# Branch a's prompt halves and three modulation tiles placed anew among four attention pairs of a decoder layer

## The chip, the cores and the metric

The kernel runs on one core of one Trainium2 chip. The metric is the device time of one execution in microseconds; the median of three runs stands for the kernel.

## The reference

One layer of a decoder, for a prompt of 256 tokens and for 8 samples of 8 new tokens that have 1024 cached tokens each. In short:

```python
mod = silu(c) @ w_ada + b_ada                       # sh1, sc1, gt1, sh2, sc2, gt2: 6 x 1024 columns
h = rmsnorm(x, g_mix) * (1 + sc1) + sh1
z = h @ w_in                                        # q, k, v, index q/k/w, retention q/k/v/gate, ga, gb
a_out = attend(...)                                 # top-k sparse attention; sample: past cache + new keys
r_out, r_state = retain(...)                        # retention, its new state is an output
merged = sigmoid(ga) * (a_out @ w_pa) + sigmoid(gb) * (r_out @ w_pb)
x = x + gt1 * (merged @ w_o)
x = x + gt2 * moe(rmsnorm(x, g_ffn) * (1 + sc2) + sh2)   # 32 experts, top 4, 12 MB of weights each
y = rmsnorm(x, g_final)
```

Branch a is `a_out @ w_pa`, branch b is `r_out @ w_pb`. All data are float32; the masks of the sample's attention are bfloat16.

## The kernel before

The program is written by hand for each engine: every engine has its own list of instructions in a fixed order, and semaphores tie the lists together. Nothing is reordered by a scheduler; the order of the code is the order of each engine and of each DMA queue. Nearly all loads are issued by SyncE, so a wait in SyncE's list holds up every load behind it.

Weights outside the experts come in tiles of 2 MB (128 partitions by 4096 words), numbered n in the order of their use: 0 to 3 modulation, 4 to 16 the input projection, 17 and 19 to 25 modulation, 18 branch a's weights (`wa`), 26 and 27 the output projection. The tiles share two buffers, `wt[0]` and `wt[1]`, in turn (`slot(n)`); `wa` lies in `wt[0]`, tiles 17, 19, 20 and 22 lie in `wt[1]`. The semaphore `tile_done` counts the matmul groups that have used a tile, in TensorE's order; `load_tile(n)` (L381 to L384) waits for this count before it overwrites a buffer. `w_here[0]` and `w_here[1]` tell TensorE that a tile has landed.

Names that the steps touch:

- `modulation_tile(n, b)` (matmuls at L1236): 16 matmuls of 512 columns (8 steps of k in 4 groups of rows that end in 32 rows each), into PSUM bank b. VectorE copies the bank into `partB[...]` (L1969 for tiles 17 and 19, L2011, `modulation_out`, for the others) and counts `partb_done`.
- `branch_a_prompt(i)` (L1248, L1249): half i (512 of 1024 columns) of branch a for the 256 prompt tokens, into banks 6 and 7. VectorE multiplies the result by the gate (L1974) and counts `ya_done`.
- `branch_a_sample()` (L1258): branch a for the 64 sample tokens, into banks 0 and 1. VectorE multiplies by the gate in four products (L2017), which also count `ya_done`.
- The sample's attention runs in four pairs i of samples. Each pair has, on TensorE, `sample_scores(i)` (L1281, and L1290 for the masks) into banks 0 to 2; `sample_prob_transposes(i)` (L1299, L1300) into banks 3, 4 and 2; `sample_values(i)` (L1313) into bank 5; and `sample_rows(i)` (L1265), a transpose of the pair's output. VectorE takes the maximum (L1961), ScalarE the exponential (L770, it counts `sexp_done`), VectorE copies the transposed probabilities (L1979, L1980, `spt_done`) and divides the output (L1987, `so_done`), ScalarE copies the output rows (L761, L762, `sa_done`).
- The scores of pair i + 1 are issued between the transposes and the values of pair i. At the head of each pair stands a piece of other work: before the change tile 17 for pair 0, branch a's half 0 for pair 1, half 1 for pair 2, tile 19 for pair 3. Tiles 17 and 19 use bank 3, so the pair's transposes wait for VectorE's copy of it.
- After the last pair follow branch a's sample half, tile 20, and then branch b (`project`, L933 to L938), whose first matmuls wait for VectorE's products on banks 0 and 1 (`ya_done` 3).

SyncE's list around this place: the load of tile 17; eight stores of the new retention state (`ret_sample`, L446), each two waiting for a count of `ns_done`; the load of tile 18, `wa`; after the first scores (`ssc2_done` 1) eight loads of 64 KB, the keys of batch row 6 (L356); tile 19; branch b's weights in two parts of 2 MB (L456), each after a pair's scores and values; tile 20; further loads that wait for the last pair. GpSimd gathers the values of the eight batch rows by indirect DMA (L582); rows 4 to 7 land where the stored state lies, so they wait for the stores (`st_out`). ScalarE issues the keys of batch row 7 in two halves, after the exponentials of pairs 0 and 1.

The expert stage streams the weights of 32 experts, six pieces of 2 MB each, through six buffers. A piece of the next expert is issued (L479, L482) when TensorE has used up the buffer (`chunk_used`).

Of the kernel before, what the change touches and what calls it, by code (L numbers as in the profile page):

```python
# [29 lines left out]
PAIRS = DB // 2  # L30
# [4 lines left out]
BANK = 512  # L35
# [111 lines left out]
def kern(nc, a):  # L147
    with ExitStack() as ctx:
# [24 lines left out]
        def bank(b, n=1):  # L173
            return ps[:, b * BANK:(b + n) * BANK]

        z3 = z[:, :].rearrange("p (t n) -> p t n", t=3)
# [185 lines left out]
        def _(sp):  # L362
# [17 lines left out]

            def load_tile(n, src, dst=None):  # L381

                sp.wait_ge(tile_done, n - 1 if n < 26 else n - 2)
                sp.dma_start(wt[slot(n)] if dst is None else dst, src).then_inc(w_here[slot(n)], 16)  # L384

            def load_modulation(n, i):
                load_tile(n, in_tile("w_ada", i))
# [52 lines left out]
            load_keys(sp, 4)  # L440
            load_keys(sp, 5)
            load_modulation(17, 4)

            for b in range(DB):
                sp.wait_ge(ns_done, b // 2 + 1)
                sp.dma_start(a["ret_sample"][b].rearrange("h d v -> d h v"),  # L446
                             state[64 * (b % 2):64 * (b % 2) + 64, b // 2, :, :]).then_inc(st_out[b // 4], 16)
            load_tile(18, a["w_branch_a"].rearrange("p (c n) -> p c n", c=4), wa)
            sp.wait_ge(ssc2_done, 1)
            load_keys(sp, 6)  # L450
            load_modulation(19, 5)
# [445 lines left out]
        def _(pe):  # L897
# [18 lines left out]
            for i in range(4):  # L916
                pe.wait_ge(w_here[i] if i < 2 else side_here[i - 2], 16)
                for k in range(KT):
                    g = k % 4
# [310 lines left out]
            def modulation_tile(n, b):  # L1230

                w = wt[slot(n)] if n < 25 else w_last
                pe.wait_ge(*tile_here(n))
                for k in range(KT):
                    g = k % 4
                    last = nc.tensor.matmul(bank(b)[32 * g:32 * g + 32, :], cT3[:, k, :], w[:, k, :],  # L1236
                                            start=k < 4, stop=k >= 4)
                last.then_inc(tile_done, 1)

            def branch_a_prompt(i):  # L1240

                if i:
                    pe.wait_ge(ya_done, 1)
                else:
                    pe.wait_ge(*tile_here(18))
                for k in range(4):
                    w = wa[:, k, i * BANK:(i + 1) * BANK]
                    nc.tensor.matmul(bank(6), aT3[:, k, 0:P], w, start=k == 0, stop=k == 3)  # L1248
                    last = nc.tensor.matmul(bank(7), aT3[:, k, P:SEQ], w, start=k == 0, stop=k == 3)  # L1249
                last.then_inc(ya_mm, 1)  # L1250
# [16 lines left out]
            def sample_scores(i):  # L1267

                pe.wait_ge(keys_here[i], 64 * NPAGES)
                if i:  # L1270
                    pe.wait_ge(sexp_done, i)
                else:
                    pe.wait_ge(z_done, NZT)
                blocks = ((0, BANK), (1, BANK), (2, DS))
                for k, w in blocks:
                    if i and k == 2:
                        pe.wait_ge(spt_done, i)
                    for h in range(2):
                        b = 2 * i + h
                        keys = kT[b][:, k * BANK:k * BANK + w] if k < 2 else kTn[:, SEQ + b * DS:SEQ + (b + 1) * DS]  # L1280
                        nc.tensor.matmul(bank(k)[NS * h:NS * h + NS, 0:w], z3[:, 2, CQ + b * NS:CQ + (b + 1) * NS],  # L1281
                                         keys, start=True, stop=False)
                if i == 0:
                    pe.wait_ge(masks_done, 1)
                    pe.wait_ge(rep_done, DB)
                    pe.wait_ge(vnew_here, 16 * DB)
                for k, w in blocks:
                    for h in range(2):
                        b = 2 * i + h
                        last = nc.tensor.matmul(bank(k)[NS * h:NS * h + NS, 0:w], rep_b[0:NS, b * NS:(b + 1) * NS],  # L1290
                                                mask_s[0:NS, k * BANK:k * BANK + w], start=False, stop=True)
                last.then_inc(ssc2_done, 1)

            def sample_prob_transposes(i):
                pe.wait_ge(sexp_done, i + 1)
                if i in (0, PAIRS - 1):
                    pe.wait_ge(partb_done, 1 + i // 3)
                for n in range(8):
                    nc.tensor.transpose(bank(3 + n // 4)[:, (n % 4) * P:(n % 4 + 1) * P], p_s[:, n:PAST:8], ident)  # L1299
                nc.tensor.transpose(bank(2)[0:DS, P:2 * P], p_s[:, PAST:KEYS], ident).then_inc(spt_tr, 1)  # L1300
# [17 lines left out]
            for i in range(PAIRS):  # L1318
                if i:
                    pe.wait_ge(spt_done, i)  # L1320
                else:
                    pe.wait_ge(rows_done, 6)
                if i in (0, PAIRS - 1):
                    modulation_tile(17 + 2 * (i // 3), 3)
                else:
                    branch_a_prompt(i - 1)
                if i:
                    sample_rows(i - 1)
                sample_prob_transposes(i)
                if i + 1 < PAIRS:  # L1330
                    sample_scores(i + 1)
                sample_values(i)
            sample_rows(PAIRS - 1)

            pe.wait_ge(sa_done, PAIRS)
            branch_a_sample()
            modulation_tile(20, 6)
            def merged_transposes(half):
                for t in range(3):
                    n = TOK[t]  # L1340
# [299 lines left out]
        def _(dve):  # L1640
# [323 lines left out]
            sample_max(0)  # L1964
            for i in range(PAIRS):

                if i in (0, PAIRS - 1):
                    dve.wait_ge(tile_done, 18 + i // 3)
                    nc.vector.tensor_copy(partB[i // 3], bank(3)).then_inc(partb_done, 1)  # L1969
                else:  # L1970
                    dve.wait_ge(ya_mm, i)
                    for t in range(2):
                        g = z3[:, t, CGA + (i - 1) * BANK:CGA + i * BANK]
                        last = nc.vector.tensor_tensor(g, bank(6 + t), g, ALU.mult)  # L1974
                    last.then_inc(ya_done, 1)
                dve.wait_ge(spt_tr, i + 1)
                if i:
                    dve.wait_ge(spv_done, i)
                nc.vector.tensor_copy(pT_s[:, 0:8, :], bank(3, 2).rearrange("p (n q) -> p n q", q=P))  # L1979
                nc.vector.tensor_copy(pT_s[0:DS, 8, :], bank(2)[0:DS, P:2 * P]).then_inc(spt_done, 1)  # L1980
                step(nc.vector.reciprocal(rs[:, i % 2:i % 2 + 1], rs[:, i % 2:i % 2 + 1]))
                if i + 1 < PAIRS:
                    sample_max(i + 1)
                dve.wait_ge(spv_done, i + 1)
                if i:
                    dve.wait_ge(sa_tr, i)
                nc.vector.tensor_scalar(o_s, bank(5)[:, 0:P], rs[:, i % 2:i % 2 + 1], None, ALU.mult).then_inc(so_done, 1)  # L1987
# [22 lines left out]
                dve.wait_ge(tile_done, 19 + i)  # L2010
                nc.vector.tensor_copy(partB[i], bank(6 + i % 2)).then_inc(partb_done, 1)  # L2011

            dve.wait_ge(tile_done, 20)
            for i in range(2):
                for h in range(2):
                    g = z3[0:NS, 2, CGA + i * BANK + h * 256:CGA + i * BANK + (h + 1) * 256]
# [310 lines left out]
```

## Time and profile before

| | us |
|---|---|
| median of 3 runs | 1473.34 |
| lowest and highest run | 1467.64, 1477.7 |
| the profiled execution's own time | 1471.61 |
| its span, first to last instruction | 1469.8 |
| TensorE busy | 1403.6 (95%) |
| VectorE busy | 512.4 (35%) |
| ScalarE busy | 218.9 (15%) |
| GpSimd busy | 69.8 (5%) |

The span is what the trace covers; the profiled execution's own time is a little longer. Busy times are sums of instructions, so an engine with a small share can still be the one that is waited for at some place. TensorE's granted clock over the span was 0.987 of its full speed. Times in the views are counted from the start of the span. In the views PE is TensorE, DVE is VectorE, ACT is ScalarE, POOL is GpSimd; SPq is SyncE's queue of DMA issues.

### The profile page before, as it was taken

Reading aid. Unit: us, or ns where it says so; the run is one execution under the profiler, and the core shown is the slowest. Engines: PE = TensorE matmul, PEld = TensorE weight load, DVE = VectorE, ACT = ScalarE, POOL = GpSimd, SP = SyncE. Lnnn points to the kernel's source line nnn. Section 1 sums busy time; section 2 is a strip of 40 time slices with the busy share of each in tenths; the row PEclk is TensorE's granted clock in tenths of the full one; section 3 lists DMA queues with packets and bytes.
Section 4 is the critical chain, followed back from the end, with each engine's and each line's share of the span. In section 5 each row is a group of like instructions: output and inputs, shape, how many; then the busy total and the mean of one; then the engine's idle time right before and its main releaser. Section 6 shows DMA issues by size and latency. Waiting matters only on the chain.

```text
span 1469.8 us, 17354 instructions
## 1 busy us (share of the span) xinstructions
PE 1403.6 (95%) x6581; PEld 584.9 (40%) x6581; DVE 512.4 (35%) x1090; ACT 218.9 (15%) x403; POOL 69.8 (5%) x67
## 2 busy tenths in 40 slices
PE   6999999998999899999999999999999999999995
PEld 3544556554445633333333333333333333333331
DVE  5133895762221522332232233213312332233125
ACT  2111222112002120111111111101111111011112
POOL 1002501141000100000000000000000000000000
PEclk9999999999999999999999999999999999999998
DMA  9424254249647369999999999999999999999992
GB/s 393 137 80 145 89 150 143 94 144 363 271 158 311 136 273 429 428 427 428 429 429 428 429 429 429 429 428 428 429 429 428 429 429 428 429 429 429 428 428 104
DMA packets 61578, 487.70 MB, mean 332 GB/s; under 512 B 8246, under 2 KB 30070, under 8 KB 32730
## 3 DMA queue, kind: packets, MB, share of 16 engines
q1 hardware_dynamic: 59226, 482.35, 79.7%
q0 software_dynamic: 1152, 4.19, 0.8%
q8 instruction: 29, 0.48, 0.1%
q10 hardware_dynamic: 1152, 0.52, 0.1%
q14 instruction: 19, 0.16, 0.0%
HBM read 482.93 MB, written 4.08 MB: 331 GB/s over the span
## 4 chain that ended last, share of the span: by engine, by line
DMA 36%; PE 34%; DVE 2%; issue 1%; ACT 0%; SPq 0%; DVEq 0%
DMA ring<-in_w_gate_up 36%; PE ps L1564 16%; PE ps L1605 5%; PE ps L1393 2%; PE ps L1511 2%; PE ps L1542 1%; PE ps L933 1%; PE ps L934 1%; PE ps L1557 1%; PE ps L1236 0%; PE ps L1348 0%; PE ps L937 0%; PE ps L1499 0%; PE ps L1587 0%; PE ps L1519 0%
## 5 line engine op out<-in xcount | busy, mean ns | idle before, releaser
L1564 PE MATMUL ps<-ring,z 128*64 128x512 f32 x2048 | 451.3, 595 | 21.1 <-DMA ring<-in_w_gate_up 21.1
L1564 PEld LDWEIGHTS ps<-ring,z 128*64 128x64 f32 x2048 | 142.2, 137 | 328.0 <-issue 278.0
L2174 DVE TENSOR_SCALAR actT<-ps 128x512 f32<-128x512 f32 x32 | 22.1, 691 | 612.6 <-PE ps L1564 612.6
L1605 PE MATMUL ps<-ring,z 128*64 128x512 f32 x1024 | 226.0, 594 | 0.0
L1605 PEld LDWEIGHTS ps<-ring,z 128*64 128x64 f32 x1024 | 72.0, 137 | 149.7 <-issue 145.5
L954 PE MATMUL ps<-ring,actT 128*128 128x512 f32 (+1 forms) x208 | 105.2, 587 | 0.0
L955 PE MATMUL ps<-ring,actT 128*128 128x512 f32 (+1 forms) x208 | 103.8, 580 | 0.0
L1511 PE MATMUL ps<-z,actT 128*64 128x512 f32 x384 | 90.6, 607 | 0.0
L1542 PE MATMUL ps<-z,aT 128*128 128x512 f32 x128 | 67.8, 631 | 2.8 <-ACT z L862 1.2
L2144 DVE TENSOR_TENSOR xr<-xr,z 128x512 f32<-128x512 f32 (+1 forms) x80 | 63.8, 797 | 2.7
L2136 DVE TENSOR_TENSOR z<-ps,z 128x512 f32<-128x512 f32 x64 | 44.1, 689 | 47.6 <-PE ps L1542 47.6
L849 ACT ACTIVATE actT<-actT 128x512 f32<-128x512 f32 x32 | 20.0, 626 | 258.9 <-DVE actT L2174 258.9
L955 PEld LDWEIGHTS ps<-ring,actT 128*128 128x128 f32 x208 | 39.5, 190 | 47.3 <-issue 45.9
L861 ACT ACTIVATE z<-ps 64x512 f32<-64x512 f32 x32 | 18.9, 589 | 248.5 <-PE ps L1605 248.5
L954 PEld LDWEIGHTS ps<-ring,actT 128*128 128x128 f32 x208 | 38.0, 190 | 41.5 <-issue 39.8
L968 PE MATMUL ps<-ring,actT 128*64 128x256 f32 (+1 forms) x208 | 46.4, 376 | 0.0
L967 PE MATMUL ps<-ring,actT 128*64 128x256 f32 (+1 forms) x208 | 46.4, 376 | 0.0
L1511 PEld LDWEIGHTS ps<-z,actT 128*64 128x64 f32 x384 | 26.6, 139 | 48.3 <-issue 47.3
L1788 DVE MAX8 st<-ring 64x8 f32<-64x1032 f32 (+2 forms) x48 | 45.0, 937 | 1.4
L1789 DVE MATCH_REPLACE8 ring<-st,ring 64x1032 f32<-64x1032 f32 (+2 forms) x48 | 44.1, 920 | 0.0
L842 ACT ACTIVATE aT<-ps 128x320 f32<-128x320 f32 x16 | 7.0, 437 | 225.5 <-PE ps L1527 225.5
L1393 PE MATMUL ps<-actT,ring 128*128 128x320 f32 x128 | 36.6, 439 | 0.0
(345 smaller groups left out, 1232.8 us busy)
## 6 DMA issues: line engine op xcount, KB each, us to landing
ring<-in_w_gate_up SPq DMA_DIRECT2D x128, 2048.0 KB, 22.9
ring<-in_w_down SPq DMA_DIRECT2D x64, 2048.0 KB, 20.6
ring<-in_w_in SPq DMA_DIRECT2D x12, 2048.0 KB, 7.8
ring<-in_w_ada SPq DMA_DIRECT2D x11, 2048.0 KB, 10.2
ring<-in_w_out SPq DMA_DIRECT2D x2, 2048.0 KB, 9.5
z<-in_cache_kT SPq DMA_DIRECT2D x40, 64.0 KB, 1.8
z<-in_w_ada SPq DMA_DIRECT2D x1, 2048.0 KB, 18.9
z<-in_cache_ikT SPq DMA_DIRECT2D x64, 32.0 KB, 2.1
```

Of the source, the lines that this page charges most:

```text
L954: nc.tensor.matmul(bank(0)[:, 0:w], hT[:, k, 0:P], wz[i][:, k, 0:w], **se)
L955: last = nc.tensor.matmul(bank(1)[:, 0:w], hT[:, k, P:2 * P], wz[i][:, k, 0:w], **se)
L967: nc.tensor.matmul(bank(2)[0:NS, 0:h], hT[:, k, 2 * P:NTOK], wz[i][:, k, 0:h], **se)
L968: last = nc.tensor.matmul(bank(2)[NS:P, 0:h], hT[:, k, 2 * P:NTOK], wz[i][:, k, h:w], **se)
L1393: last = nc.tensor.matmul(bank(6 + c % 2)[:, 0:NTOK], w[:, k, c % 4 * P:(c % 4 + 1) * P], hT[:, k, :], start=k == 0, stop=k == KT - 1)
L1511: last = nc.tensor.matmul(bank(3)[64 * i:64 * i + 64, :], S[:, t, :], h2[:, t, i * BANK:(i + 1) * BANK], start=t == 0, stop=t == 2)
L1542: nc.tensor.matmul(bank(b), SgT[:, t * P:(t + 1) * P], ysb[buf][:, half * BANK:(half + 1) * BANK], start=True, stop=True).then_inc(cmb_mm, 1)
L1564: done = nc.tensor.matmul(bank(q // 2)[64 * (q % 2):64 * (q % 2) + 64, :], lhs, ring3[k // 2][:, (k % 2) * 2048 + q * BANK:(k % 2) * 2048 ...
L1605: done = nc.tensor.matmul(bank(2)[64 * q:64 * q + 64, :], lhs, ring3[4 + k // 4][:, (k % 4) * D + q * BANK:(k % 4) * D + (q + 1) * BANK], ...
L1788: step(nc.vector.max(m8, v))
L1789: step(nc.vector.match_replace(v, m8, v, TAKEN))
L2144: last = nc.vector.tensor_tensor(acc[0:n, t, c], acc[0:n, t, c], tmp3[0:n, t, c], ALU.add)
```

## The change

TensorE's order among the pairs becomes: pair 0: tile 17 and branch a's half 0; pair 1: half 1; pair 2: tile 19 at its head; pair 3: nothing at its head, and tile 20 between its transposes and its values, where other pairs have the next pair's scores. VectorE's list follows. Since tile 20 now comes before branch a's sample half, its count `tile_done` 20 and 21 change places: VectorE waits for 21 before the four products, and the load of tile 21, which overwrites `wa`, waits for 21 too. In SyncE's list the load of `wa` moves ahead of the eight stores.

```diff
@@ -380,7 +380,7 @@
             def load_tile(n, src, dst=None):
 
-                sp.wait_ge(tile_done, n - 1 if n < 26 else n - 2)
+                sp.wait_ge(tile_done, 21 if n == 21 else n - 1 if n < 26 else n - 2)
@@ -440,12 +440,12 @@
             load_modulation(17, 4)
+            load_tile(18, a["w_branch_a"].rearrange("p (c n) -> p c n", c=4), wa)
 
             for b in range(DB):
                 sp.wait_ge(ns_done, b // 2 + 1)
                 sp.dma_start(a["ret_sample"][b].rearrange("h d v -> d h v"),
                              state[64 * (b % 2):64 * (b % 2) + 64, b // 2, :, :]).then_inc(st_out[b // 4], 16)
-            load_tile(18, a["w_branch_a"].rearrange("p (c n) -> p c n", c=4), wa)
@@ -1293,8 +1293,8 @@
             def sample_prob_transposes(i):
                 pe.wait_ge(sexp_done, i + 1)
-                if i in (0, PAIRS - 1):
-                    pe.wait_ge(partb_done, 1 + i // 3)
+                if i in (0, 2):
+                    pe.wait_ge(partb_done, 1 + i // 2)
@@ -1320,21 +1320,22 @@
-                if i in (0, PAIRS - 1):
-                    modulation_tile(17 + 2 * (i // 3), 3)
-                else:
-                    branch_a_prompt(i - 1)
+                if i in (0, 2):
+                    modulation_tile(17 + i, 3)
+                if i < 2:
+                    branch_a_prompt(i)
                 if i:
                     sample_rows(i - 1)
                 sample_prob_transposes(i)
                 if i + 1 < PAIRS:
                     sample_scores(i + 1)
+                else:
+                    modulation_tile(20, 6)
                 sample_values(i)
             sample_rows(PAIRS - 1)
 
             pe.wait_ge(sa_done, PAIRS)
             branch_a_sample()
-            modulation_tile(20, 6)
@@ -1964,13 +1965,13 @@
-                if i in (0, PAIRS - 1):
-                    dve.wait_ge(tile_done, 18 + i // 3)
-                    nc.vector.tensor_copy(partB[i // 3], bank(3)).then_inc(partb_done, 1)
-                else:
-                    dve.wait_ge(ya_mm, i)
+                if i in (0, 2):
+                    dve.wait_ge(tile_done, 18 + i // 2)
+                    nc.vector.tensor_copy(partB[i // 2], bank(3)).then_inc(partb_done, 1)
+                if i < 2:
+                    dve.wait_ge(ya_mm, i + 1)
                     for t in range(2):
-                        g = z3[:, t, CGA + (i - 1) * BANK:CGA + i * BANK]
+                        g = z3[:, t, CGA + i * BANK:CGA + (i + 1) * BANK]
@@ -2010,7 +2011,7 @@
-            dve.wait_ge(tile_done, 20)
+            dve.wait_ge(tile_done, 21)
```

SyncE's list behind the keys of batch row 5 and tile 17 (both at its head here), as a difference. L355 is the head of the loads of row 6's keys.

```order
 L356 DMA ring<-in_cache_kT 128x128
 L384 DMA ring<-in_w_ada 128x4096 [waits tile_done]
-L446 DMA ret_sample<-ring 64x8x128 [waits ns_done] x8
 L384 DMA ring<-in_w_branch_a 128x4096 [waits tile_done]
+L447 DMA ret_sample<-ring 64x8x128 [waits ns_done] x8
 L355 TENSOR_LOAD pt [waits ssc2_done]
 L355 ISA x2
```

The eight stores stand behind branch a's weights instead of ahead of them; the waits in the list are the same.

TensorE's list at the head of pair 3, from the last instruction ahead of it on, as a difference: L1236 is a modulation tile (tile 19 where it is taken out, tile 20 where it is put in), L1265 the rows of pair 2, L1299 and L1300 pair 3's transposes, L1313 its values.

```order
-L1236 MATMUL ps<-ring,cT 32x512 [waits w_here1,spt_done]
-L1236 MATMUL ps<-ring,cT 32x512 x7
-L1265 MATMUL ps<-cst,ring 128x128 [waits so_done]
-L1299 MATMUL ps<-cst,ring 128x128 [waits partb_done,sexp_done]
+L1265 MATMUL ps<-cst,ring 128x128 [waits so_done,spt_done]
+L1299 MATMUL ps<-cst,ring 128x128 [waits sexp_done]
 L1299 MATMUL ps<-cst,ring 128x128 x7
 L1300 MATMUL ps<-cst,ring 8x128
+L1236 MATMUL ps<-ring,cT 32x512 [waits w_here1]
+L1236 MATMUL ps<-ring,cT 32x512 x7
 L1313 MATMUL ps<-ring 64x128 [waits gathered7,sa_done,gathered6,spt_done]
 L1313 MATMUL ps<-ring 64x128 x17
```

The head of the pair is empty, and a modulation tile stands between transposes and values.

TensorE's list from branch a's sample half (L1258) to the first matmuls of branch b (L933, L934), as a difference.

```order
 L1258 MATMUL ps<-ring,aT 64x256 [waits sa_done]
 L1258 MATMUL ps<-ring,aT 64x256 x15
-L1236 MATMUL ps<-ring,cT 32x512 [waits w_here1]
-L1236 MATMUL ps<-ring,cT 32x512 x7
 L933 MATMUL ps<-z,actT 128x512 [waits ya_done,side_here0]
 L934 MATMUL ps<-z,actT 128x512
```

Branch b follows branch a's sample half directly.

## Rows read from the trace of the kernel before

**Rows 1.** The chain of waits, whole program: start us, us, what it was.

```profile
521.02 13.88 PE ps L1564 x64
...
1405.25 25.88 DMA ring<-in_w_gate_up
```

**Rows 2.** Stretches: length, busy time by engine (instructions), granted clock, DMA share, GB/s.

```profile
342.00:346.00 4.00, 4.00 (x18) 1.33 (x18) 1.48 (x3) 0.00 (x0) 0.00 (x0) 0.57 1.04 389
...
379.00:383.00 4.00, 3.02 (x28) 3.03 (x30) 0.99 (x3) 0.00 (x0) 0.00 (x0) 0.60 0.94 399
...
815.00:1435.00 620.00, 598.94 (x2778) 203.96 (x2775) 167.42 (x347) 76.96 (x137) 0.00 (x0) 1.00 1.01 428
```

**Rows 3.** SyncE's queue in order of time: start us, us, line, transfer, count.

```profile
329.27 0.35 SPq L384 DMA_DIRECT2D ring<-in_w_branch_a  x1
338.92 8.07 SPq L356 DMA_DIRECT2D z<-in_cache_kT  x8
347.03 0.44 SPq L384 DMA_DIRECT2D ring<-in_w_ada  x1
...
361.63 0.80 SPq L456 DMA_DIRECT2D ring<-in_w_branch_b  x2
376.38 0.33 SPq L384 DMA_DIRECT2D ring<-in_w_ada  x1
...
524.79 10.62 SPq L479 DMA_DIRECT2D ring<-in_w_gate_up  x4
```

**Rows 4.** TensorE in order of time: start us, us, line, operation, count, idle before.

```profile
335.92 1.92 PE L1236 MATMUL ps<-ring,cT 128*32 128x512 f32 x16 [1.66 <-ACT actT L752]
340.89 1.16 PE L1299 MATMUL ps<-cst,ring 128*128 128x128 f32 x8 [3.05 <-ACT ring L770]
...
342.10 3.61 PE L1281 MATMUL ps<-z 128*64 128x512 f32 x8
...
361.47 1.13 PE L1248 MATMUL ps<-ring,aT 128*128 128x512 f32 x2
...
368.44 0.27 PE L1265 MATMUL ps<-cst,ring 128*128 128x128 f32 x1
...
372.14 2.33 PE L1313 MATMUL ps<-ring 128*64 128x128 f32 x36
374.40 1.92 PE L1236 MATMUL ps<-ring,cT 128*32 128x512 f32 x16
...
377.23 1.14 PE L1299 MATMUL ps<-cst,ring 128*128 128x128 f32 x8 [0.65 <-DVE xr L1969]
...
379.98 3.87 PE L1313 MATMUL ps<-ring 128*64 128x128 f32 x36 [1.50 <-DVE ring L1980]
384.36 0.33 PE L1265 MATMUL ps<-cst,ring 128*128 128x128 f32 x1 [0.51 <-DVE ring L1987]
385.23 3.67 PE L1258 MATMUL ps<-ring,aT 128*64 128x256 f32 x32 [0.54 <-ACT aT L762]
...
390.92 1.10 PE L933 MATMUL ps<-z,actT 128*128 128x512 f32 x2 [0.16 <-DVE z L2017]
```

**Rows 5.** The stores of the retention state (line 446): shortest, median and longest issue.

```profile
L446 SPq DMA_DIRECT2D ret_sample<-ring x8: 596/766/2667, 311.4 to 327.6; - x8
```

**Rows 6.** DMA issues, whole program: count, KB each, median us from issue to landing.

```profile
ring<-in_w_branch_a SPq DMA_DIRECT2D x1, 2048.0 KB, 10.9
...
ring<-in_cache_v,irow POOLq DMA_INDIRECT x6, 11.5
```

**Rows 7.** DMA issues of 376 to 377 us: the load of tile 20.

```profile
ring<-in_w_ada SPq DMA_DIRECT2D x1, 2048.0 KB, 8.2
```

**Rows 8.** VectorE in order of time, at pair 0 and behind the last pair.

```profile
338.17 1.23 DVE L1961 TENSOR_REDUCE st<-ps 128x1 f32<-128x1032 f32 x1 [10.44 <-remote]
...
389.05 1.72 DVE L2017 TENSOR_TENSOR z<-ps,z 64x256 f32<-64x256 f32 x4 [4.74 <-PE ps L1258]
```

**Rows 9.** The page's first line.

```profile
span 1469.8 us, 17354 instructions
```

## The prediction

> **What bounds the kernel now.** I started at the end. The chain of waits closes with a weight transfer of 25.9 us for every expert [rows 1], and from 815 to 1435 us the sixteen DMA engines have a share of 1.01 at 428 GB/s [rows 2]. The expert stage moves 31 experts of 12.6 MB after the first, which is 909 us at that rate. Counted back from 1435 us, that is 526 us, and the queue issues the second expert's first piece at 524.8 us [rows 3], as soon as TensorE, which begins the first expert at 521.0 us [rows 1], has finished with that piece's buffer. So the weight stream has one start, set by TensorE, and no slack after it: a microsecond that the front gains or loses comes out at the end, one for one.
>
> Before that, TensorE is the chain. In the stretch that the change touches, from the end of the first modulation tile (tile 17, 335.92 + 1.92 = 337.84 us) to the first matmul of branch b at 390.92 us, lie 53.1 us [rows 4]. The reader is to see four kinds of time in it. (1) Waits: 3.05 us for ScalarE's exponential ahead of pair 0's transposes; in the last pair 0.65 us for VectorE's copy of tile 19, 1.50 us for the copy of the transposed probabilities, 0.51 and 0.54 us in the step from the last values to branch a's sample rows; 0.16 us ahead of branch b. Together 6.4 us. (2) A lower clock: the granted share is 0.57 in 342 to 346 us and 0.60 in 379 to 383 us [rows 2], both right behind a stretch with waits, which costs 4 x 0.43 = 1.7 and 4 x 0.40 = 1.6 us; the rows show it, since one pair's eight 512-column score matmuls take 3.61 us there [rows 4]. (3) Work at the full clock, the rest, 43.4 us, which the change only orders anew. (4) Pairs 1 and 2 run without a wait of TensorE: a half of branch a (361.47 to 368.44, 6.97 us) covers VectorE's and ScalarE's softmax, and the pair takes 374.40 - 361.47 = 12.93 us, of which 2.26 us are its values (372.14 to 374.40) [rows 4].
>
> **The change, part by part.** I lay out the new time line from 337.84 us.
>
> Branch a's weights. The name says "ahead of stores", but the load waits for tile 17 of the count, the last tile of the input projection, and that is what released it before as well: it goes out at 329.27 us, 0.35 us long, while the last store had begun at 327.6 [rows 3, 5]. So the weights are not issued earlier; the eight stores are issued later, from 329.6 us. What the weights gain is a queue with nothing ahead. They took 10.9 us, beside the gathers of the values and two stores [rows 6]; a load of the same 2 MB into an empty queue took 8.2 us [rows 7]. So they land between 337.5 and 340.2 us. Without the two stores (0.5 MB, some 1.2 us at 428 GB/s) but with the gathers still beside them I take 338.5 us, a wait of 0.7 us (bounds 0 and 2.4).
> The Trainium skill (DMA: Bandwidth & Descriptors, "Anatomy of one DMA — SWDGE (gpsimd) path") gives a fit of 2.0 us plus the bytes over 436 GB/s, for the path from GpSimd. By that the weights would land 6.8 us after their issue, before tile 17 is through, and the sum would be 0.7 us lower. The same page ("Queues, rings and completion order") says that each DMA engine takes its queue rows in turn, which speaks against it: the gathers take their share whatever stands ahead in the other queue. The trace's 8.2 us for an empty queue decides for the slower price.
>
> Pair 0. Half 0 of branch a (6.97 us) now runs in the gap of 3.05 us. The exponential is ready at 340.9 us, long before the half ends. The wait of 3.05 us becomes 0.7: **-2.35 us**. Since no wait of that size is left there, I expect the low clock of 342 to 346 us to go: **-1.7 us**. VectorE gets two products (1.3 us) ahead of its copies here; pairs 1 and 2 had the same ones before and did not wait, so: nothing.
>
> The pairs then end so: pair 0 at 338.5 + 12.93 = 351.4 us (values 0 done), pair 1, with half 1, at 364.3 us.
>
> Pair 2. Tile 19 stands where half 1 stood. Its cost moves with it (1.9 us), and so does the wait of 0.65 us for its copy: 0 net. It needs its weights by 364.3 us; I come to them below. Transposes, scores and values take 12.93 - 6.97 = 5.96 us, so the values end at 364.3 + 1.9 + 0.3 + 0.65 + 5.85 = 373.0 us.
>
> Pair 3. Nothing stands ahead of the transpose of pair 2's output rows now, so TensorE waits for VectorE's division, which modulation work covered before. The same step behind the last pair cost 0.51 us [rows 4]: **+0.5 us**. The exponential (some 2.8 us after the scores, as in pair 0 from VectorE's maximum at 338.17 us [rows 8] to TensorE's start at 340.89) is ready by then, covered by 2.3 us of values and this wait. After the transposes, at 375.0 us, tile 20 covers VectorE's copy: **-1.5 us**. But tile 20's weights are issued only once tile 19 is done, at 366.2 us, and behind 2 MB of branch b's that go out when values 1 are done, at 364.3 us. Lower bound: they land 8.2 us after their issue [rows 7], at 374.4, no wait. Upper bound: 8.2 us for branch b's 2 MB, then 4.9 us at 428 GB/s, 377.4, a wait of 2.4 us. The 2 MB ahead are certain, so I take a value nearer the upper end, **+1.5 us**. Before, this load had from 376.38 us [rows 3] to 385.23 + 3.67 = 388.9 us [rows 4], the end of branch a's sample half, to land.
>
> Behind the pairs. Tile 20 used to run between branch a's sample half and branch b. In that time VectorE did the four products that free PSUM banks 0 and 1: 389.05 us, 1.72 us [rows 8]. TensorE now has nothing to do meanwhile: the wait of 0.16 us becomes 2.0 us, **+1.8 us**. The next loads (21 and on) still wait for branch a's sample half, so they move with it.
>
> Low clock of 379 to 383 us: the waits around the last pair (0.5 + 1.5 us) are about what they were (0.65 + 1.50), so one such stretch stays: 0.
>
> **Sum:** -2.35 - 1.7 + 0.5 - 1.5 + 1.5 + 1.8 = -1.75 us, against the profiled execution's 1471.61 us (span 1469.8 us [rows 9] and 1.8 us around it). That is 1469.9 us; the median of the runs is 1.7 us above that execution, so in terms of the median 1473.34 - 1.75 = 1471.6 us.
>
> Work hidden, and what hides it. The gathers of pairs 2 and 3 write over the stored states, so they wait for the stores: these land 7 to 8 us after their issue and behind the weights, by some 347 us; with 11.5 us for a gather [rows 6] the values are there by 362 us, and values 2 begin at 370.7. Cover 9 us. ScalarE's second half of pair 3's keys moves back by 3 us with the exponential; they are wanted at 368 us.
>
> **Rivals.** *The stores block the queue (slower).* SyncE issues, behind the stores, the keys of batch row 6 (8.07 us for eight), and then tile 19 [rows 3]. A store's issue took 0.6 to 2.67 us, median 0.77 [rows 5]. By the median eight are through at 335.8 us, before the keys' own release at 338.9: no delay. By the longest they last until 351 us, tile 19 is issued at 359.1 and lands at 367.3 to 370, so pair 2 waits 3 to 6 us. Tile 19 is late once a store takes over (364.3 - 8.2 - 8.1 - 329.6) / 8 = 2.3 us. For it: the long ones were those issued into a backlog, and here 2 MB are ahead, with the gathers beside them. Against it: only one of eight was that long. This gives -1.75 + 4.5, 1476 us; chance 0.15.
>
> *The clock stays high (faster).* If neither low stretch is left, another 1.6 us go, and with the weights in time 0.7 more: 1469.3 us. For it: waits are in smaller pieces. Against it: 0.65 and 1.50 us were enough before. Chance 0.15.
>
> *More low clock (no gain).* A low stretch stays behind pair 0, or the new wait of 2.0 us makes one in branch b's first tile, 1.7 us each: 1473.3 to 1475 us. Chance 0.25.
>
> *The change doesn't do what it says:* half 0 isn't moved into the gap because its weights come later than 340.9 us, the old end of the wait. Then half 0 follows the old wait, and only the rest counts: about 1474 us, chance 0.03.
>
> **How the numbers follow.** My forecast, one low stretch gone and the moved waits as priced, has 0.42. All cases lie between 1468 and 1478 us, within 0.4% of the median, while the three runs shown spread by 0.7%. So the range takes the cases and some of that spread: 1466 to 1478.5 us. A measurement of this kernel can tell about 1% from no change, which is 14.7 us. None of the cases reaches it; I leave 0.03 for faster and 0.03 for slower, for effects that this trace doesn't hold.
>
> **What would show it right or wrong.** In the changed kernel's trace: branch a's weights issued at about 329.3 us and landed by 339; no wait of 3 us ahead of pair 0's transposes, clock 1.00 around 342 to 346 us; tile 20's first matmul waiting some 1.5 us for its weights; 2.0 us in front of branch b, released by VectorE's products; branch b at some 389.2 us, and the second expert's first piece issued 1.75 us earlier than 524.8. It is wrong if the stores take more than 2.3 us each to issue, if low clock covers more than one stretch, or if the start of the stream moves and the end doesn't.

## The result, and the profile after

| | before | after |
|---|---|---|
| median of 20 runs each | 1473.82 | 1477.74 |
| lowest and highest | 1467.64, 1477.70 | 1472.53, 1483.27 |
| ratio of the times, 95% interval | | 1.0033 [1.0022, 1.0044] |
| span of the profiled execution | 1469.8 | 1475.6 |

The changed kernel is 3.9 us slower where 1.75 us less were forecast; the interval leaves out 1, so the loss is clear of the noise of this comparison. Times in this text are us; "before" and "after" are the two kernels.

TensorE of after, in order of time; the bracket at a row's end is the idle time ahead of it and what ended it:

```profile
336.77 1.92 PE L1236 MATMUL ps<-ring,cT 128*32 128x512 f32 x16
342.72 2.08 PE L1248 MATMUL ps<-ring,aT 128*128 128x512 f32 x2 [4.03 <-DMA ring<-in_w_branch_a]
...
371.36 1.92 PE L1236 MATMUL ps<-ring,cT 128*32 128x512 f32 x16
...
374.19 1.13 PE L1299 MATMUL ps<-cst,ring 128*128 128x128 f32 x8 [0.65 <-DVE xr L1970]
...
380.73 0.30 PE L1265 MATMUL ps<-cst,ring 128*128 128x128 f32 x1 [0.54 <-DVE ring L1988]
...
384.64 1.92 PE L1236 MATMUL ps<-ring,cT 128*32 128x512 f32 x16 [2.60 <-DMA ring<-in_w_ada]
...
395.90 1.68 PE L933 MATMUL ps<-z,actT 128*128 128x512 f32 x2 [2.02 <-DVE z L2018]
```

These answer to [rows 4]. The reader is to see that the wait of pair 0 that was to go has come back in another form. Half 0 waits 4.03 for branch a's weights. Tile 20, which was to cover a wait of 1.50 in the last pair, waits 2.60 for its own weights. The terms that needed no transfer came as priced: 0.54 ahead of the rows of pair 2, 0.65 for tile 19's copy, 2.02 ahead of branch b. Tile 19 itself (371.36) waits for nothing.

Stretches of after, in the layout of [rows 2]:

```profile
342.00:344.00 2.00, 1.28 (x2) 0.77 (x3) 0.00 (x0) 0.00 (x0) 0.00 (x0) 0.50 1.04 367
344.00:346.00 2.00, 2.00 (x3) 0.75 (x3) 0.00 (x0) 0.00 (x0) 0.00 (x0) 0.50 1.15 344
346.00:348.00 2.00, 2.00 (x3) 0.67 (x2) 0.00 (x0) 0.00 (x0) 0.00 (x0) 0.50 1.14 336
348.00:350.00 2.00, 2.00 (x6) 0.94 (x5) 0.00 (x0) 0.00 (x0) 1.42 (x2) 0.88 1.05 292
...
360.00:370.00 10.00, 10.00 (x57) 5.12 (x58) 3.38 (x6) 0.44 (x2) 0.00 (x0) 1.00 0.98 403
370.00:380.00 10.00, 9.35 (x104) 5.49 (x100) 4.59 (x9) 2.15 (x5) 0.00 (x0) 1.00 0.84 308
396.00:400.00 4.00, 4.00 (x6) 1.70 (x7) 0.47 (x1) 0.00 (x0) 0.00 (x0) 0.57 1.02 417
```

Behind the wait of 4.03 the granted clock is at the lower level (0.50, that is 1.2 of 2.4 GHz) through most of half 0, which takes 9.8 instead of 6.97, so 2.85 are lost there; half 1 behind it is at 1.00. A second low stretch lies in branch b's first matmuls, 4 x 0.43 = 1.7. In before the stretches 360 to 380 look like this:

```profile
360.00:370.00 10.00, 10.00 (x54) 5.40 (x52) 2.50 (x6) 1.65 (x4) 0.00 (x0) 1.00 0.57 215
370.00:380.00 10.00, 7.85 (x82) 4.27 (x78) 5.23 (x10) 1.65 (x4) 0.00 (x0) 0.99 0.28 81
```

Before had slack in its DMA engines there (shares 0.57 and 0.28); after has little (0.98, 0.84). Whether this is what makes tile 20 late is settled by e1, below: it isn't.

SyncE's queue of after, which answers to [rows 3]:

```profile
331.85 0.34 SPq L384 DMA_DIRECT2D ring<-in_w_branch_a  x1
332.24 15.52 SPq L447 DMA_DIRECT2D ret_sample<-ring  x8
349.24 8.40 SPq L356 DMA_DIRECT2D z<-in_cache_kT  x8
357.68 0.46 SPq L384 DMA_DIRECT2D ring<-in_w_ada  x1
358.59 2.02 SPq L456 DMA_DIRECT2D z<-in_w_branch_b  x2
371.52 1.62 SPq L456 DMA_DIRECT2D ring<-in_w_branch_b  x2
373.35 0.33 SPq L384 DMA_DIRECT2D ring<-in_w_ada  x1
...
531.45 10.62 SPq L479 DMA_DIRECT2D ring<-in_w_gate_up  x4
```

The issues of after at 331.85 and at 373.35, with KB each and time to landing, against 10.9 [rows 6] and 8.2 [rows 7]:

```profile
ring<-in_w_branch_a SPq DMA_DIRECT2D x1, 2048.0 KB, 10.8
...
ring<-in_w_ada SPq DMA_DIRECT2D x1, 2048.0 KB, 11.3
```

GpSimd of after, gather 4, which waits for the stores; in before all eight gathers are issued by 336.4:

```profile
348.28 0.94 POOL L582 DMA_INDIRECT ring<-in_cache_v,irow  x1 [14.28 <-DMA ret_sample<-ring]
```

**The ledger.** I call the region what lies between TensorE's first L1224 (branch a's weights are issued within 0.1 of it) and its first matmul of branch b. For it before takes 390.92 - 329.17 = 61.75 and after 395.90 - 331.74 = 64.16, +2.4. With the low stretch behind it, in branch b, +4.1, which is the size of the median's +3.9. Pair 0 has a small part in it: its waits went from 1.66 + 3.05 to 4.03 (-0.68) and its low clock from 1.7 to 2.85 (+1.15), +0.5 together. The rest, +3.6, lies from pair 3 on: 0.54 for the rows of pair 2, 1.1 at tile 20, 1.86 ahead of branch b and 0.1 of low clock. The spans differ by 5.8 because the stretch ahead of the change, the same instructions in both, ended 2.57 later in this execution; from the first piece of the stream to the end lie 945.0 and 944.15.

### The profile page after: what moved, and what is told of

It reads as the page before. It is cut to its first block, busy times and chain, and to the rows that moved or that the text cites. A ratio compares the mean times of both kernels' runs of the same rounds, so it can differ in the third digit from the quotient of the medians.

```text
span 1475.6 us, 17354 instructions
## 1 busy us (share of the span) xinstructions
PE 1404.9 (95%) x6581; PEld 585.7 (40%) x6581; DVE 512.5 (35%) x1090; ACT 218.9 (15%) x403; POOL 69.9 (5%) x67
## 4 chain that ended last, share of the span: by engine, by line
PE 54%; DMA 41%; DVE 2%; issue 1%; ACT 1%; SPq 0%; DVEq 0%
DMA ring<-in_w_gate_up 38%; PE ps L1565 15%; PE ps L954 6%; PE ps L955 6%; PE ps L1606 5%; PE ps L967 3%; PE ps L1394 2%; DMA ring<-in_w_in 2%; PE ps L1512 2%; PE ps L1543 1%; PE ps L933 1%; PE ps L934 1%; DMA ring<-in_w_branch_a 1%; PE ps L1558 1%; DMA ring<-in_w_ada 1%
```

## The experiments

They ran on three chips, P, Q and R here, each beside the kernel before on the same chip. Its medians there: 1473.07 (P), 1468.75 and 1468.81 (Q, two batches), 1468.56 (R). In the expectations A is the theory that the time is lost in TensorE's new order: in the wait for branch a's weights, in the wait for tile 20's, and in the clock behind them. B puts it down to the stores behind branch a's weights, C to the gathers that run beside these weights. Where an expectation gives a letter a narrower sense, its own words hold. Labels that say "third chip" were given before the chip was known; s1 to s4 ran on Q.

**Stores first again (chip P).** In the changed kernel:

```diff
-            load_tile(18, a["w_branch_a"].rearrange("p (c n) -> p c n", c=4), wa)
             for b in range(DB):
...
+            load_tile(18, a["w_branch_a"].rearrange("p (c n) -> p c n", c=4), wa)
```

> The changed kernel with one part undone: the eight stores are issued ahead of branch a's weights again; TensorE's order is the new one. Theory A (the place of the matmul work costs the time: the weights land some 10.8 us after their issue whatever the order in the queue, because the gathers run beside them, and tile 20 stands in a bad place): no better than the changed kernel, 1477 to 1479 us, ratio to before 1.002 to 1.004, TensorE's wait for branch a's weights 4 us or more. Theory B (the new order of SyncE's queue costs it, since stores and weights now share the same time): 1474 us or less.

1476.84, ratio to before 1.0025 [1.0005, 1.0045]. Half 0 still waits 2.95, and in front of tile 17 stand 1.58 again; the weights take 11.4 with the stores ahead of them. TensorE at tile 20, the issue of tile 20's weights, and the stretch before:

```profile
386.26 3.64 PE L1236 MATMUL ps<-ring,cT 128*32 128x512 f32 x16 [3.67 <-DMA ring<-in_w_ada]
```

```profile
ring<-in_w_ada SPq DMA_DIRECT2D x1, 2048.0 KB, 12.3
```

```profile
360.00:370.00 10.00, 10.00 (x49) 4.89 (x49) 2.82 (x6) 0.44 (x2) 0.00 (x0) 1.00 0.62 237
370.00:380.00 10.00, 9.35 (x108) 5.72 (x106) 5.13 (x9) 1.65 (x4) 0.00 (x0) 1.00 0.71 267
```

So the order in SyncE's queue is not what costs. Nor do the stores and gathers that the new order pushes back: here all are early and the engines have slack (shares 0.62 and 0.71), and tile 20's weights, behind the same 2 MB of branch b, still land after 12.3 and are waited for 3.67. In e4, with the stores early too, they take 11.8.

**Only the queue (P, and R).** In the kernel before, the load moved ahead of the stores and nothing else.

> The kernel before with only the queue changed: branch a's weights ahead of the eight stores, TensorE's order as before. Theory A: no change, ratio 0.999 to 1.001, since half 0 runs at 348 us and its weights are there at 343. Theory B: 2 to 4 us slower than before, because the keys, tile 19 and the gathers come some 8 us later.

1469.51 on P, 0.9970 [0.9951, 0.9988]: faster, which neither theory had. Its gap ahead of pair 0's transposes is 0.92, not the 3.05 of before. On R:

> The queue-only kernel once more (TensorE's order of before, branch a's weights ahead of the stores). If its gain is real: ratio to before 0.9965 to 0.998, and 6 to 9 us below the changed kernel. If the first result was chance: 0.999 to 1.001.

1468.33, 0.9998 [0.9981, 1.0015], and the same 0.92. The gain is there on P alone, where before itself is 4.5 slower than on R.

**Tile 20 back (P).** In the changed kernel, tile 20 behind branch a's sample half, with its counts; and the same with the stores first.

```diff
-                else:
-                    modulation_tile(20, 6)
                 sample_values(i)
...
             branch_a_sample()
+            modulation_tile(20, 6)
```

> The changed kernel with tile 20 put back behind branch a's sample half, so that the last pair has no tile at all; the queue's order and branch a's halves as in the changed kernel. Theory A: the wait of 2.60 us behind the last transposes becomes the copy's 1.50, the wait of 2.02 us ahead of branch b becomes 0.16, and the low clock in branch b's first matmuls (1.7 us) goes: 4.7 us faster than the changed kernel, 1473 us, ratio to before 0.999 to 1.000. Rival (the loss sits in pair 0 alone): 1476 to 1478 us.

1470.63, 1.0001 [0.9981, 1.0021]. Half 0 waits 4.30, the copy's 1.50 is back, tile 20 waits for nothing and branch b for 0.16.

> Both undone: tile 20 behind branch a's sample half and the stores ahead of branch a's weights; only the two prompt halves and tile 19 keep their new places. Theory A: as with tile 20 alone put back, 1473 us within 1 us. Theory B: 3 us or more below that run.

1471.90, 0.9982 [0.9964, 1.0001]. Half 0 waits 2.54 and runs at the full clock. This run and e1 differ in tile 20's place alone: it is 4.9 less by the medians, 6.3 by the ratios. So most of the loss comes with tile 20's move, and half 0's move gains nothing that is clear of noise (1.0001, 0.9982).

**All gathers held until branch a's weights are in (Q).** In the changed kernel, ahead of the first gather:

```diff
+                if b == 0:
+                    pool.wait_ge(*tile_here(18))
```

> The changed kernel with GpSimd's eight gathers held back until branch a's weights have landed; all else as in the changed kernel. Theory C (the weights land 10.8 us after their issue because the gathers take their share of the DMA engines): landing 8.2 to 8.7 us, TensorE's wait for them 1.4 to 2.0 us where it was 4.03, and less of half 0 at the low clock; 2 to 5 us faster than the changed kernel, ratio to before 1.000 to 1.002. Rival (the stores behind the weights, or the memory's own pace, slow them): landing 10 us or more, no gain.

1474.85, 1.0049 [1.0032, 1.0066]; the changed kernel has 1.0033 in the first comparison and 1.0068 on R, so no gain is shown. The weights land 9.1 after their issue. TensorE:

```profile
344.08 1.13 PE L1250 MATMUL ps<-ring,aT 128*128 128x512 f32 x2 [2.31 <-DMA ring<-in_w_branch_a]
...
377.60 3.68 PE L1283 MATMUL ps<-z 128*64 128x512 f32 x8 [3.66 <-DMA z<-in_cache_kT]
```

C is right on the landing, if not on its size (8.2 to 8.7 were expected): without the gathers beside them the weights take 1.7 less, and half 0 keeps the full clock. But now pair 3's keys are waited for, and the low clock stands there. That the gathers, moved back, hold them up is argued from their order, not isolated.

**Work in the wait (Q).** In the changed kernel, tile 17's 16 matmuls three times over, each time from a fresh start, so that TensorE is busy while the weights come:

```diff
+                for r in range(3 if n == 17 else 1):
                     for k in range(KT):
```

> The changed kernel with tile 17's 16 matmuls run three times instead of once (same operands, same bank, same result), so that TensorE works through most of its wait for branch a's weights. Theory D (half of the loss in pair 0 is the low clock that follows the wait: half 0 took 9.8 us where 6.97 is its time at the full clock): the wait shrinks from 4.03 to under 1 us, half 0 takes 7.0 to 7.5 us, 2 to 3 us faster than the changed kernel, ratio 1.001 to 1.002. Rival (the low clock does not depend on the wait): half 0 stays at 9 to 10 us, time as the changed kernel's or worse.

1477.03, 1.0073 [1.0046, 1.0100]. TensorE:

```profile
336.11 5.36 PE L1237 MATMUL ps<-ring,cT 128*32 128x512 f32 x48
342.16 1.12 PE L1249 MATMUL ps<-ring,aT 128*128 128x512 f32 x2 [0.69 <-DMA ring<-in_w_branch_a]
...
383.35 3.64 PE L1237 MATMUL ps<-ring,cT 128*32 128x512 f32 x16 [4.71 <-DMA ring<-in_w_ada]
```

and the stretch ahead of that wait:

```profile
370.00:380.00 10.00, 7.44 (x74) 4.96 (x73) 5.19 (x9) 2.08 (x6) 0.00 (x0) 1.00 1.00 416
```

With busy time in front, half 0's matmuls run at the full clock (1.12 instead of 2.08 for two), so the low clock there comes with the wait. What pair 0 gains, tile 20 hands back: its weights take 13.4, in a stretch with full DMA engines (1.00, 416 GB/s), and low clock follows their wait.

**Before once more (R, Q).**

> The kernel before itself, for its trace on this chip. In the three traces so far with the stores ahead of branch a's weights, ScalarE and VectorE are released 3 to 4 us late in pair 0 and TensorE waits 1.5 to 1.7 us ahead of tile 17; in those with the weights ahead, or the gathers held, neither. Theory G' (this belongs to the order of before whatever the chip): 1.6 us ahead of tile 17 and 3 us for the exponential again. Rival (it belongs to a chip or an execution): none ahead of tile 17 and 0.9 us for the exponential.

> The kernel before once more, one look at its trace. Theory D1 (the late release of ScalarE and VectorE in pair 0 belongs to one execution or one chip): the gap ahead of pair 0's transposes is 0.92 us on some chips and 3.05 on others, with nothing in the list of instructions that tells them apart; either may come here. Theory D2 (it comes with gathers 4 to 7 issued beside the softmax): it should be 3.05 us, with some 1.6 us ahead of tile 17, as in the first trace.

1465.37 on R and 1462.81 on Q, one execution each. TensorE of before on R:

```profile
334.63 1.92 PE L1236 MATMUL ps<-ring,cT 128*32 128x512 f32 x16
337.47 1.16 PE L1299 MATMUL ps<-cst,ring 128*128 128x128 f32 x8 [0.92 <-ACT ring L770]
```

The same kernel without a wait ahead of tile 17 and with 0.92 for the exponential, on Q too. ScalarE of the first trace of before, and of the one on R:

```profile
332.33 0.60 ACT L752 ACTIVATE actT<-ps 128x512 f32<-128x512 f32 x1 [0.68 <-PE ps L1224]
335.20 0.66 ACT L752 ACTIVATE actT<-ps 128x256 f32<-128x256 f32 x2 [2.27 <-remote]
```

```profile
330.51 2.62 ACT L752 ACTIVATE actT<-ps 128x512 f32<-128x512 f32 x6
```

In the first trace ScalarE stood 2.27 for a release that the trace puts down to no engine ("remote"), between copies that run through on R; VectorE's maximum was released by "remote" as well [rows 8]. The region takes 61.75 in the first trace of before, 384.26 - 329.60 = 54.66 on R and 385.47 - 330.82 = 54.65 on Q. The difference of 7.1 is 1.66 ahead of tile 17, 3.05 - 0.92, and the two low stretches, 1.7 + 1.6, which R and Q don't have.

**Before with gathers 4 to 7 held until pair 0's exponential (Q, twice).**

```diff
+                if b == 4:
+                    pool.wait_ge(sexp_done, 1)
```

> The kernel before, its queue order and TensorE's order untouched, with one wait added on GpSimd: gathers 4 to 7 are issued only when pair 0's exponential is done. Theory G (in the kernel before, the gathers that GpSimd issues while TensorE does pair 0's scores hold up the release of ScalarE and VectorE by 3 to 4 us, and the queue-only run gained because its later stores held these gathers back): TensorE's wait of 1.66 us ahead of tile 17 is gone, the wait for the exponential is 0.9 us instead of 3.05, 4 to 5 us faster than before, ratio 0.9965 to 0.998. Rival S (the gain of the queue-only run comes from the order of stores and weights in SyncE's queue itself): the waits stay at 1.66 and 3.05 us and the time is before's.

1468.85, 1.0000 [0.9982, 1.0018]; gap 0.92.

> The kernel before with gathers 4 to 7 held until pair 0's exponential. Theory D2: the gap ahead of pair 0's transposes is 0.92 us although the kernel before shows 3.05 on this chip, and the time is some 3 to 4 us less. Theory D1: gap as in the kernel before on the same chip, time the same within 1 us.

1469.28, 0.9994 [0.9973, 1.0014]; gap 0.92. It makes no difference on Q, where before is without the gap too. D2 falls in its plain form: gathers 4 to 7 run beside the softmax on R and Q, and the late release isn't there. It was seen in three traces, the first one and e1 and e4 on P, all with the stores first, and in none of e2 and e3 on P. Chip and gathers together would fit; before wasn't traced again on P, so it stays open.

**The changed kernel once more (R).**

> The changed kernel itself beside the queue-only kernel on one chip, since the ratio to before of the held gathers (1.000) and of the queue-only run (0.997) come from two chips. Ratio to before 1.003 to 1.005; TensorE's wait for branch a's weights 4 us, half 0 at the low clock for a part, tile 20 waiting 2.5 to 3.5 us, 2.0 us ahead of branch b.

1477.55, 1.0068 [1.0047, 1.0090]. TensorE:

```profile
345.03 2.07 PE L1248 MATMUL ps<-ring,aT 128*128 128x512 f32 x2 [4.76 <-DMA ring<-in_w_branch_a]
...
387.29 2.73 PE L1236 MATMUL ps<-ring,cT 128*32 128x512 f32 x16 [2.97 <-DMA ring<-in_w_ada]
```

The changed kernel's time is that of the first comparison (1477.74); what differs is before, whose median is 5.3 less here. Against r1 the region is 66.85 - 54.66 = 12.2 longer: waits of 12.0 instead of 4.3, and 4.5 of low clock.

**Tile 20's weights ahead of branch b's second part (Q).** In the changed kernel's loop over branch b's parts:

```diff
+                if i:
+                    load_modulation(20, 6)
...
-            load_modulation(20, 6)
```

> The changed kernel with tile 20's weights issued ahead of the second part of branch b's weights instead of behind it. Theory A (tile 20 is late because of the transfers ahead of it): it lands some 8.2 to 9 us after its issue instead of 11.3, TensorE's wait for it goes from 2.6 to 3 us to at most 0.5, and the time is 2 to 3 us below the changed kernel's, so 1.5 to 4 us above the kernel before. Rival (the whole stretch is full, by stores and gathers that were pushed back): it lands 11 us after its issue as before, the wait stays above 1.5 us, and the time is that of the changed kernel.

1472.49, 1.0044 [1.0025, 1.0064]. TensorE at branch a's half 0 and at tile 20, and the issue of tile 20's weights:

```profile
342.87 2.07 PE L1249 MATMUL ps<-ring,aT 128*128 128x512 f32 x2 [4.14 <-DMA ring<-in_w_branch_a]
...
380.99 1.92 PE L1237 MATMUL ps<-ring,cT 128*32 128x512 f32 x16
```

```profile
ring<-in_w_ada SPq DMA_DIRECT2D x1, 2048.0 KB, 8.6
```

A holds in its narrow form: 8.6 instead of 11.3, and no wait for tile 20, in a stretch as full as that of after. Above before it is 3.7 by the medians, as expected, and 6.5 by the ratio, of which r2's was 10.0. The two intervals overlap, so the landing and the wait are shown and the gain in time isn't. The wait of 4.14 and its low clock are still in it.

**Tile 19 between the last pair's transposes and values (Q, R, Q).** The kernel before with the queue of e2, and tile 19 in bank 7 where it covers the copy's 1.50:

```diff
                 if i + 1 < PAIRS:
                     sample_scores(i + 1)
+                else:
+                    modulation_tile(19, 7)
                 sample_values(i)
```

> A version meant to be better: the queue-only run (TensorE's order of before, branch a's weights ahead of the stores) with tile 19, instead of tile 20, between the last pair's transposes and values, in PSUM bank 7; its weights land long before. The waits of 0.65 and 1.50 us in the last pair go, one of 0.5 us for the rows of pair 2 comes, the low clock behind them (1.6 us) may go, tile 20 may wait up to 1 us for its weights: 1 to 3 us faster than the queue-only run, ratio to before 0.995 to 0.9965. Rival (these waits are made up elsewhere): as the queue-only run, 0.997.

> Tile 19 between the last pair's transposes and values, weights ahead of the stores, on the same chip as the two above. The trace of its first run had the waits of 0.65 and 1.50 us gone and 1.55 us for tile 20's weights instead: 1 to 2 us below the queue-only kernel if what it saves reaches the end, equal to it if it is made up elsewhere.

> The kernel before with branch a's weights ahead of the stores and tile 19 between the last pair's transposes and its values. It had 0.9999 and 0.9986 on two chips. If it is faster than the kernel before it should be 0.998 to 0.999 here too (some 2 us less, or up to 4 us less where the kernel before shows the gap of 3.05 us); if not, 1.000.

1467.02, 0.9999 [0.9983, 1.0015]; 1465.92, 0.9986 [0.9971, 1.0002]; 1463.30, 0.9969 [0.9954, 0.9983]. Two of the three are on one chip and their intervals barely meet, so two batches of one kernel differ by more than an interval says. Its waits of 0.65 and 1.50 are gone, one of 0.55 for the rows of pair 2 has come, but tile 20 then waits (1.55, 0.74, 2.61), and in the last run with a low clock:

```profile
383.62 2.91 PE L1236 MATMUL ps<-ring,cT 128*32 128x512 f32 x16 [2.61 <-DMA ring<-in_w_ada]
```

It may be some 2 faster than before (the mean of the three ratios is 0.9985); that isn't settled. Nor is it shown to beat the queue's change alone (0.9970 and 0.9998) or e4 (0.9982).

## Why the prediction was wrong

The forecast failed in its sign; 1477.74 lies inside the range given. By its own steps:

- **Branch a's weights: -2.35.** The step that failed first. The forecast took 9.2 from issue to landing; it was 10.8 (11.6 on R), what the row of before had said [rows 6]. Its own subtraction, 10.9 less 1.2 for the two stores, gives 9.7; the further 0.5 had no reason. Only the 9.1 of e5, without gathers, reaches the forecast value. The second error is in when TensorE would be there: the forecast started from tile 17's end at 337.84 in a trace that has 1.66 ahead of tile 17. That wait fell away in after, so TensorE was there earlier and waited for the same landing. 1.66 + 3.05 became 4.03: -0.68, a miss of 1.67. By the fit of the Trainium skill (DMA: Bandwidth & Descriptors, "Anatomy of one DMA — SWDGE (gpsimd) path"), which is for loads that GpSimd issues, the estimate was 6.8. No load of 2 MB in these stretches landed in under 7.8, and branch a's weights never in under 9.1. What shortened their landing was holding all gathers (9.1), not leaving out the stores ahead (10.8 against 10.9), nor holding gathers 4 to 7 alone (10.9 and 11.0, e9 and s2). The Trainium skill (DMA: Bandwidth & Descriptors, "Queues, rings and completion order") has each DMA engine take its queue rows in turn, and the traces agree: work in another queue slows the load whatever stands ahead in its own.
- **Low clock behind pair 0: -1.7.** It was +1.15: a wait of 4.03 stood in front of half 0, and the clock was low over more than half of it. This is the largest miss, 2.85, and follows from the first: e5 and e6, with waits of 2.31 and 0.69, have no low clock there. Its size isn't set by the wait: half 0 lost 2.85 behind 4.03, 1.7 behind 4.14 (s3) and 1.4 behind 4.30 (e3).
- **Rows of pair 2: +0.5.** 0.54. Right.
- **Tile 20: -1.5 and +1.5.** The copy's wait went; the weights' wait was 2.60 (2.97 on R), 0.2 above the bound of 2.4. The upper bound had it right: issued at 366.2 and landed at 377.4 are 11.2, measured 11.3. What failed was the choice of 1.5 between the bounds, though the 2 MB ahead were called certain. s3 shows that they decide: without them 8.6 and no wait. Miss 1.1.
- **Branch b: +1.8.** 2.02 - 0.16 = +1.86. Right.
- **Low clock of 379 to 383: 0.** It went (-1.6) and another came in branch b (+1.7). Right in sum, by luck in its place: the forecast kept it at the last pair. On R none stood in branch b, and one behind tile 20 instead.
- **The stream moves one for one.** Right but for 0.9: its first piece was 6.66 later, the span 5.8 longer. In its working 31 x 12.6 MB at 428 GB/s are 913, not 909; the start counted back is then 522 and the argument stands.

The misses, 1.67 + 2.85 + 1.1 + 0.1 = 5.7, make +3.95 of -1.75; measured +3.9. That the sum closes this well is partly luck, since executions of one kernel spread by 10. The forecast's own sign of being wrong, low clock in more than one stretch, was met.

**The rivals.** The stores took 15.5 / 8 = 1.9 each on average, under the 2.3 that was given, and tile 19 was in time; with the stores first the time is the same (e1). "More low clock" was the nearest in mechanism: both of its stretches came, in pair 0 and in branch b, but at 2.85 + 1.7 instead of 1.7 each, and the one at the last pair, which it kept, went. "The change doesn't do what it says" wanted the weights later than 340.9. They landed at 342.65 in a trace in which they were issued 2.58 later, which is 340.1 on the forecast's time line, so its condition was just missed.

**What no step held.** The gap of 3.05, the gain's whole ground, was read from one execution. On Q and R it is 0.92. On R the same change costs 9.0 instead of 3.9 (medians of r2).

## What to carry to other kernels

A gap is worth filling with work whose operands are there when it opens: compare the landing of the weights, as measured beside the same traffic, with the moment the gap opens, not with the moment it ends. When work moves ahead, look at what stands directly ahead of its weights in the queue: tile 20's landed after 11.3 behind 2 MB and after 8.6 without them. When transfers are held back for one wait, list what comes behind them: with the gathers held, the wait moved from half 0 to pair 3's keys. Before a gap is counted on, look for it in a second trace of the same kernel, above all one whose releaser no engine of the trace accounts for.

## What the runs showed of the hardware

- **The same waits, with and without a low clock.** In e2 the last pair's values take 3.83 behind waits of 0.65 and 1.50; in r3, the same program, they take 2.33 behind the same waits. The 2.02 ahead of branch b had a low clock behind it in after, and none in r2 and s3. Behind single waits of 2.61 to 4.76 one followed each time (s4, e1, r2, before, e5, after, s3, e3, e6), behind 2.31 to 2.60 never (e5, e4, after). The wait's length alone doesn't decide it, as 1.50 and 2.02 show, and it doesn't set how long the clock stays low: behind half 0's wait it lasted from 342.7 to 348.5 in after (4.03), and from 342.9 to 346.4 in s3 (4.14).
- **A release with no engine behind it**, 2.24 to 2.27 on ScalarE, in the first trace of before, e1 and e4, and in neither of two further traces of before. Its cause is open.
- **The same load of 2 MB took very different times**: tile 20's 8.0 to 8.2 with an empty queue (before, r1, s1), 8.6 ahead of branch b's 2 MB (s3), 11.3 to 12.3 behind them (after, r2, e1, e3, e4), 13.4 and 13.7 behind them in stretches at 416 and 422 GB/s (e6, e5). Branch a's weights took 9.1 without gathers and 9.9 to 11.6 beside them.
- **One kernel's median moved by 5 between comparisons, another's not**: before has 1473.8 in the first comparison and 1473.1 on P, but 1468.6 to 1468.8 on Q and R; the changed kernel has 1477.7 in the first comparison and 1477.6 on R. Whether the chip does it isn't shown.
